# Block-doubling inverse of the chunk recurrence: each level on half of its columns

## What is computed

```python
def step(S, inp):
    r_t, w_t, k_t, v_t, kk_t, b_t = inp
    Sa = jnp.einsum('bhij,bhj->bhi', S, -kk_t)
    S = S * w_t[:, :, None, :] + Sa[..., None] * b_t[:, :, None, :] + v_t[..., None] * k_t[:, :, None, :]
    return S, jnp.einsum('bhij,bhj->bhi', S, r_t)
```

## Time and profile before

| | us |
|---|---|
| median of 3 runs | 1726.22 (1724.63 to 1727.69) |
| profiled execution | 1722.33, its span 1720.5 |
| recurrence of layer 1, first PE row to the start of the tail's last products | 458 to 628 of the span |
| the same of layer 2 | 1296 to 1469 |
| one undisturbed turn (546.62 to 561.70) | 15.08 |
| PE, DVE, ACT, POOL busy over the span | 92%, 59%, 49%, 34% |

### The profile page before, as it was taken

The page is one execution under the profiler, slowest core; times in us unless marked ns, Lnnn a source line. Parts: engine busy times, 40 slices in busy tenths (PEclk is TensorE's granted clock), DMA queues, the critical chain, the costliest instruction groups (busy, mean ns, idle before and its releaser), DMA issues. The chain is left out here.

```text
span 1720.5 us, 41466 instructions
## 1 busy us (share of the span) xinstructions
PE 1581.8 (92%) x17389; PEld 1499.4 (87%) x17389; DVE 1009.6 (59%) x1718; ACT 843.4 (49%) x1480; POOL 578.6 (34%) x393
## 2 busy tenths in 40 slices
PE   4999999989799899999789999999897989899996
PEld 4999999987588789999789999989776878899995
DVE  3534368695798665443354434968677877544433
ACT  2545455756444555444344444656663446554431
POOL 0433412102266433444233433020215553344440
PEclk9999999999899999999989999999998999999998
DMA  5555557452144445555355555644603463456540
GB/s 174 161 173 177 177 151 220 129 173 79 48 121 124 138 155 176 169 195 178 112 158 173 178 176 183 194 134 145 184 1 101 128 182 101 148 172 196 178 166 26
DMA packets 280490, 256.28 MB, mean 149 GB/s; under 512 B 48022, under 2 KB 268540, under 8 KB 280290
## 3 DMA queue, kind: packets, MB, share of 16 engines
q1 hardware_dynamic: 276538, 252.05, 47.0%
q10 hardware_dynamic: 3768, 1.59, 0.4%
HBM read 242.22 MB, written 11.38 MB: 147 GB/s over the span
## 5 line engine op out<-in xcount | busy, mean ns | idle before, releaser
L223 PE MATMUL ps<-front_h_hi,front_hi 128*128 128x264 f32 x1520 | 447.4, 294 | 35.1 <-DVE front_lo L210 31.2
L224 PE MATMUL ps<-front_h_lo,front_hi 128*128 128x264 f32 x1520 | 436.9, 287 | 0.0
L225 PE MATMUL ps<-front_h_hi,front_lo 128*128 128x264 f32 x1520 | 436.5, 287 | 0.0
L210 POOL TENSOR_TENSOR front_lo<-front_raw,front_hi 128x1024 fp32r<-128x1024 f32 (+2 forms) x90 | 217.5, 2416 | 574.2 <-ACT front_hi L203 574.2
L203 ACT ACTIVATE front_hi<-front_raw 128x1024 fp32r<-128x1024 f32 (+2 forms) x238 | 246.7, 1039 | 274.7 <-PE ps L225 237.0
L223 PEld LDWEIGHTS ps<-front_h_hi,front_hi 128*128 128x128 f32 x1520 | 291.6, 192 | 44.8 <-issue 41.2
L210 POOL TENSOR_TENSOR out_lo<-out_raw,out_hi 128x1024 fp32r<-128x1024 f32 (+1 forms) x84 | 198.8, 2369 | 310.8 <-ACT out_hi L203 310.8
L224 PEld LDWEIGHTS ps<-front_h_lo,front_hi 128*128 128x128 f32 x1520 | 291.9, 192 | 0.8
L225 PEld LDWEIGHTS ps<-front_h_hi,front_lo 128*128 128x128 f32 x1520 | 290.2, 191 | 0.1
L203 ACT ACTIVATE out_hi<-out_raw 128x1024 fp32r<-128x1024 f32 (+1 forms) x168 | 173.2, 1038 | 220.9 <-PE ps L225 178.0
L210 DVE TENSOR_TENSOR front_lo<-front_raw,front_hi 128x1024 fp32r<-128x1024 f32 (+1 forms) x148 | 180.0, 1217 | 118.7 <-ACT front_hi L203 118.7
(11 more groups left out here) (375 smaller groups left out, 3346.9 us busy)
## 6 DMA issues: line engine op xcount, KB each, us to landing
front_raw<-in_w_in SPq DMA_DIRECT2D x50, 1024.0 KB, 5.3
front_raw<-in_ffn_w_in SPq DMA_DIRECT2D x44, 1024.0 KB, 5.7
out_raw<-in_ffn_w_in SPq DMA_DIRECT2D x44, 1024.0 KB, 5.6
back_sample_rows<-row_scratch SPq DMA_DIRECT2D x160, 128.0 KB, 3.0
out_raw<-in_w_out SPq DMA_DIRECT2D x16, 1024.0 KB, 6.3
front_raw<-in_ffn_w_out SPq DMA_DIRECT2D x16, 896.0 KB, 4.6
out_raw<-in_ffn_w_out SPq DMA_DIRECT2D x16, 896.0 KB, 4.6
front_raw<-in_ffn_w_out SPq DMA_DIRECT2D x8, 1024.0 KB, 5.0
```

Source lines behind the costliest of these rows:

```text
L210: eng.tensor_tensor(self.lo[n % self.RING][:, 0:k, 0:w], self._raw(n), self.hi[n % self.RING][:, 0:k, 0:w].bitcast(F32), ALU.subtract).the ...
L223: pe.matmul(out, hi[:, j, 0:w], x_hi[:, j], start=start and j == 0, stop=False)
L224: pe.matmul(out, hi[:, j, 0:w], x_lo[:, j], start=False, stop=False)
L225: mm = pe.matmul(out, lo[:, j, 0:w], x_hi[:, j], start=False, stop=stop and j == k - 1)
```

## The change

`part_of(a, i, late)` takes the 256 columns of a tile as groups of 2b and gives the first b of each (late = 0) or the last b (late = 1), 128 columns in all. At level i only the first half of each group changes in x, and only the second half in xt. So:

- all three products of a level have 32 moving columns instead of 64, written to 32 columns of each PSUM block with the same stride;
- the ACT copy and both DVE additions work on 128 elements per partition instead of 256, in runs of b elements;
- T is now zero outside of the copied half, and must be so where it is a weight. So `n_x` becomes five tiles, one per level (`t1_pair` for two, `t1_rest` for three), which POOL clears once per layer by two MEMSETs of 512 and 768 elements; for pair 0 ACT waits for them (`t1_zero`). The second MEMSET stands in turn 1 of POOL ahead of level 1 of pair 0, behind a wait for `tok_ps`, since its place held factors of pair 0.

The number of matmuls, copies and additions is the same, as are all waits but `t1_zero`.

```diff
--- before.py
+++ after.py
@@ -1461,6 +1461,12 @@
 
 
     LV, V = len(LEVELS), 5
+
+    def part_of(a, i, late):
+        b = LEVELS[i]
+        return a.rearrange("p (n two t) -> p n two t", two=2, t=b)[:, :, late]
+
+    columns = lambda a: a.rearrange("p q t -> p (q t)")
     KK, DEC, MB, KEY, REC = range(V)
     with Stage(nc, f"back{layer}") as st:
         s, ps, at = st.s, env.ps, mix.place
@@ -1478,12 +1484,14 @@
         lev = st.sb("n_levels", [P, 2, 4, C])
         x = st.sb("inverse", [P, 2, 4, C])
         xt = st.sb("inverse_t", [P, 3, 4, C])
-        t1 = st.sb("n_x", [P, 4, C])
+        t1_pair = st.sb("n_x_first", [P, 2, 4, C])
+        t1_rest = at("n_x_rest", 71296, [P, LV - 2, 4, C])
         rw = st.sb("gv_a", [P, 2, 4, 2, C])
         uw = st.sb("u_w", [P, 4, 2, C])
         carry = st.sb("carry", [P, NCH, C])
         read = st.sb("read_out", [P, NCH, C])
         state_at = st.sb("states", [P, NCH, C])
+        t1 = lambda i: t1_pair[:, i] if i < 2 else t1_rest[:, i - 2]
         vecs, last = mix.vecs, mix.last
         root, sc_root = mix.root, mix.sc_root
         sh_rows = at("shift_new_rows", 0, [9, 4, SC])
@@ -1616,8 +1624,12 @@
                     c = slice(2 * q, 2 * q + 2)
                     pool.tensor_tensor(short_lo[:, c], mix.ys[:, c], short_hi[:, c].bitcast(F32), ALU.subtract).then_inc(s("short_lo"), 1)
 
+                pool.memset(t1_pair[:], 0.0).then_inc(s("t1_zero"), 1)
                 for g in range(RT + 1):
                     l = g - 1
+                    if g == 1:
+                        pool.wait_ge(s("tok_ps"), 2)
+                        pool.memset(t1_rest[:], 0.0).then_inc(s("t1_zero"), 1)
                     if l >= 0:
                         level(l, 1)
                     if g < RT:
@@ -1672,7 +1684,9 @@
                     act.wait_ge(s("t1_ps"), n + 1)
                     if n:
                         act.wait_ge(s("ut_ps"), n)
-                    act.activation(t1[:].rearrange("p q t -> p (q t)"), ps[:, T1B, 0:4 * C], ACT.Copy).then_inc(s("t1_in"), 1)
+                    if p == 0:
+                        act.wait_ge(s("t1_zero"), 1 if i < 2 else 2)
+                    act.activation(part_of(columns(t1(i)), i, 0), part_of(ps[:, T1B, 0:4 * C], i, 0), ACT.Copy).then_inc(s("t1_in"), 1)
 
                 def x_copy(p):
                     act.wait_ge(s("x_ps"), p + 1)
@@ -1873,18 +1887,19 @@
                                       ALU.add).then_inc(s("start"), 1)
 
                 def update(p, i):
-                    four = lambda b: ps[:, b, 0:4 * C].rearrange("p (q t) -> p q t", q=4)
                     if i < LV - 1:
                         dve.wait_ge(s("u_ps"), (LV - 1) * p + i + 1)
                         if i:
                             dve.wait_ge(s("x_up"), (LV - 1) * p + i)
                         else:
                             dve.wait_ge(s("x_in"), p + 1)
-                        dve.tensor_tensor(x[:, p % 2], x[:, p % 2], four(UB), ALU.add).then_inc(s("x_up"), 1)
+                        changed = part_of(columns(x[:, p % 2]), i, 0)
+                        dve.tensor_tensor(changed, changed, part_of(ps[:, UB, 0:4 * C], i, 0), ALU.add).then_inc(s("x_up"), 1)
                     dve.wait_ge(s("ut_ps"), LV * p + i + 1)
                     if i:
                         dve.wait_ge(s("xt_up"), LV * p + i)
-                    dve.tensor_tensor(xt[:, p % 3], xt[:, p % 3], four(UB + 1), ALU.add).then_inc(s("xt_up"), 1)
+                    changed = part_of(columns(xt[:, p % 3]), i, 1)
+                    dve.tensor_tensor(changed, changed, part_of(ps[:, UB + 1, 0:4 * C], i, 1), ALU.add).then_inc(s("xt_up"), 1)
 
                 def transfer(p):
                     by_chunk = lambda a: a.rearrange("p (c o) t -> p o c t", o=2)
@@ -2053,10 +2068,12 @@
                                                    start=True, stop=True)
                     mm.then_inc(s("g_ps"), 1)
 
-                def blocks(at, left, right):
+                def blocks(at, left, right, i, late):
+
                     for q in range(4):
                         for w in half:
-                            mm = pe.matmul(ps[w, at, q * C:(q + 1) * C], left[w, q], right[w, q], start=True, stop=True)
+                            mm = pe.matmul(part_of(ps[w, at, q * C:(q + 1) * C], i, late), left[w, q], part_of(right[w, q], i, late),
+                                           start=True, stop=True)
                     return mm
 
                 def turn_x(p):
@@ -2076,7 +2093,7 @@
                         pe.wait_ge(s("t1_in"), n)
                     else:
                         pe.wait_ge(s("x_in"), p + 1)
-                    blocks(T1B, lev[:, n % 2], x[:, p % 2]).then_inc(s("t1_ps"), 1)
+                    blocks(T1B, lev[:, n % 2], x[:, p % 2], i, 0).then_inc(s("t1_ps"), 1)
 
                 def level_u(p, i):
                     n = LV * p + i
@@ -2084,8 +2101,8 @@
                     if n:
                         pe.wait_ge(s("xt_up"), n)
                     if i < LV - 1:
-                        blocks(UB, xt[:, p % 3], t1[:]).then_inc(s("u_ps"), 1)
-                    blocks(UB + 1, t1[:], xt[:, p % 3]).then_inc(s("ut_ps"), 1)
+                        blocks(UB, xt[:, p % 3], t1(i), i, 0).then_inc(s("u_ps"), 1)
+                    blocks(UB + 1, t1(i), xt[:, p % 3], i, 1).then_inc(s("ut_ps"), 1)
 
                 def gv(p):
```

## The result

The changed kernel is slower: 1733.32 us against 1725.11 us for the kernel before (medians of 19 runs each, taken side by side). The ratio is 1.0046, 95% interval 1.0033 to 1.0059: 8 us of loss where 11 us of gain were forecast. The profiled execution took 1731.52 us, its span 1729.6 against 1720.5.

A forecast was written before the change was run, and what follows sets the result against it. PE was taken as nearest the bound (13.7 us of a turn), DVE close behind at 13.55. Matmuls gaining nothing, shorter PE waits gave 9.5 to 14.4 us, taken as 11.2: 1726.2 to 1715 us, own range 1711 to 1721, overall 1697 to 1724.

The forecast's parts named there:

- The matmuls cost the same at 32 columns as at 64: Level blocks on PE, 14 a pair: no gain from 64 to 32 moving columns, 0.47 us from start to start.
- A: Rival: level matmuls on PE follow their columns, a block falls to 0.27 us; 1690 to 1704 us, chance 0.22.
- C: Rival: PE stumbles over short runs of moving and output columns; slower, 1734 us, or 1752 with runs of 4; chance 0.08.
- Copy 274 ns, additions 286 ns: Halved copy of T on ACT and additions on DVE: gain 0.11 us a copy and 0.13 us an addition.
- MEMSETs hidden: Zeroing of the T tiles on POOL, about 0.53 and 0.75 us, falls into idle time and costs nothing.
- The copy's waits down by 5 us: PE's 43 weight-load waits for ACT's copy of T, 18.0 us in all, shrink by 4.6 us.
- The 37 waits ahead of a block, 4.9 to 9.8 us: PE's weight-load waits on issue before level blocks, 19.8 us, shrink by 4.9 us, or 9.8 behind two additions.
- The sum, 11 us: Whole kernel: shorter copy and issue waits together 9.5 to 14.4 us, taken as 11 us.

The follow-up runs named there:

- thin rows: Sample-row loads from pair 1 on fill 4 partitions of each half instead of 64: kernel before 1716.40 us; wide products with short copies and additions 1713.15 us.

## Why the prediction was wrong

- **The matmuls cost the same at 32 columns as at 64: right but for 0.03 us a block.** 0.49 us from block to block at full clock against 0.52 (the 0.47 of the earlier trace rows was the fast end of what 64 columns take), far from A's 0.27. Where the 0.03 us went doesn't show: with pairs 1 to 7 wide or narrow the times are the same. Rival A is out, and so is C as I told it: no stumbling over short runs. The Trainium skill, page "PSUM — Partial Sum Buffer", section "Specifications (TRN2)", had it that any pattern which isn't contiguous slows matmuls significantly; the output in runs of 2 to 16 float32 values, at 0.44 to 0.49 us from block to block, doesn't show it.
- **Copy 274 ns, additions 286 ns: right**, within 3%, but for the copy at level 0 (289 ns). **MEMSETs hidden: right**, since the kernel with wide products has them and its first turns took 28.11 and 27.88 us.
- **The copy's waits down by 5 us: right** (18.0 to 13.7).
- **The 37 waits ahead of a block, 4.9 to 9.8 us: wrong, the mis-sized term.** The waits measured 20.9 us after where 19.8 less 4.9 to 9.8 was forecast, and 17.2 against 18.4 with thin rows. I had called most of them waits for x or for the level mask, and a few unexplained stops, and then priced all 37 as if each ended with an addition.
- **The sum, 11 us: wrong.** Where clock and traffic are taken out, 3.3 us came, hardly clear of the noise; the undisturbed turn gave 0.3 us, inside the 14.3 to 14.8 us that the prediction named for it, but under the 0.35 us that it named as the least gain. Where the rest of the shortened work's time stays (masks, PE's own queue) was not taken apart.
- **The step that failed, and that turned the sign: no term for the clock.** I read 0.98 and 0.97 in the earlier trace rows and 1.00 in the earlier trace rows and went on with full clock for the whole stage. The trace held a warning: the clock of the kernel before falls for 3.4 us in layer 2's first turn, right where in layer 1 show PE standing still for 2.02 us between short groups. A saving that has next to no effect on PE's time could still have an effect on its clock, and did: 17 us at 1.2 GHz in each layer, 10.4 us in the two first turns. The 8.8 us between the two traces are that, less 4.6 us in turns two to six and eight, and 3.0 us more in the seventh, where the burst of loads is and where the clock fell for longer as well (0.83 in both layers, 0.91 and 1.00 before).
- **C's sign was right, its mechanism wrong.** "Slower" had a chance of 0.08, and the range ended at 1724, while the median came to 1733. That C had 1734 us as its price is luck: it is the sum of a loss that doesn't exist (no undisturbed block took over 0.49 us at full clock) and a gain that mostly didn't come.

The Trainium skill, page "TensorE: Matmul & The Clock Gate", section "HAM oscillation — how this bites in real kernels", tells of a kernel whose few matmuls between two waits for DMA are shorter than the wait, so that its clock falls back each time. The trace agrees in so far as the clock fell in a thin stretch, behind a gap of 2.03 us. But it doesn't explain the difference: the same gap between wide blocks left it up in layer 1 of the kernel before, and with the narrow products issued twice it fell behind a gap of 0.62 us. No run here shows where the border lies.

## What to carry to other kernels

Making these matmuls narrower, from 64 to 32 columns, bought 0.03 us a block on TensorE and no time that shows, and where TensorE had little to do it cost the clock; before such an edit look for the stretches where PE stands still between short groups, and leave the products there whole. A wait labelled "issue" is not a wait for the operation you shorten until its releaser is known; count only those that are proved. And a few short stops of PE near a burst of large transfers may be worth as much as the edit: spreading three loads gave 4.5 us, all the shortened copies and additions together 3.3 to 4.5.

## What the runs showed of the hardware

- Twice as many narrow matmuls, with PE busy for 4.38 of the 5 us from 470 us on, were followed by 1.2 GHz (0.50 in 478 to 500 us); as many with every second one wide ran at 0.99. The busy share of a stretch at the lower level is no sign of load: 97 to 98% there, since its rows take nearly twice as long.
- A fall can outlast by far what stood ahead of it: 17 us behind a gap of 2.03 us in the changed kernel, 24 us behind one of 0.62 us with doubled narrow blocks. With wide products at the same place it was none, 3.4 us or, in two traces, 10.2 us.
- Short runs cost ACT next to nothing: 289 ns a copy with runs of 2, 275 ns with runs of 4, 273 ns with 8 to 32. DVE's additions took 279 to 288 ns at every level.
- With the DMA engines at 330 to 380 GB/s, 128 KB transfers landed in 6.3 us, over the whole stage in 3.1, and PE stopped for 1.4 to 2.7 us where the profile shows nothing to wait for; with the rows' traffic cut from 136 to 85 GB/s the kernel before ran 9 us faster.
